# Taking one vector-matrix product off TensorE: ScalarE scales its rows, GpSimd adds them, and the weights are loaded later

## The chip, the cores and the metric

The kernel runs on one core of a Trainium2 chip. The metric is the device time of one execution, in microseconds; lower is better. All tensors are float32 in memory.

## The reference, cut to what matters

The program computes one layer of a hybrid attention block with a mixture of 32 experts, and behind it two layers of a second model, on 256 tokens of width 1024. The part that the change touches is the modulation:

```python
mod = (jax.nn.silu(c) @ w_ada + b_ada).reshape(b, 6, 1, 1024)
shift1, scale1, gate1, shift2, scale2, gate2 = (mod[:, i] for i in range(6))
h = rms_norm(x, norm1_g) * (1 + scale1) + shift1
x = x + gate1 * (y @ w_out)                       # y: the three mixers' output
h2 = rms_norm(x, norm2_g) * (1 + scale2) + shift2
```

`c` is one vector of 1024, `w_ada` is 1024 x 6144. The "second modulation" is columns 2048 to 4095 of the product: gate1 and shift2. gate1 is needed when the attention output has been projected, shift2 in the router and in the experts' inputs.

## The kernel before, in words

Every weight comes through a ring of 16 slots of 128x2048 floats (`ring`). `ring_order()` gives each load (a "unit") its slot; SyncE issues the loads in one fixed order (`fill`), each after waiting for what empties its slot (`emptied`). The slots 8 to 13 hold the split copies of the first stage and are not loaded into there; 14 and 15 are free until the experts.

The first stage ("front") computes `h @ w_in` in 32 pieces. A piece `n` is 256 rows of one block of columns: ScalarE makes its rounded high part (`hi`, in `his`), VectorE the rest (`lo`, in `los`, a subtraction of two SBUF inputs), and TensorE multiplies with both (`project(n)`, three products each, 12 to a half). `land(b)` copies a finished block out of PSUM. The attention mixers are woven between the pieces: `head_turn`, `cumulate` (the running sum of the forget gates `lf`), `sb_z`, `sb_r`, `sb_w` for the six stick-breaking heads, `fx_z`, `fx_t`, `fx_w` for the six forgetting heads. ScalarE and VectorE do their logarithms, exponentials and masks (`sb_beta`, `fx_mask`), GpSimd multiplies by the strict mask (`strict`) and by the convolution's taps (`tapped`). The order on each engine is written out by hand, an engine never goes on before its current wait is over, and counting semaphores (`done(name)`) join them.

The modulation is done in the same stage. `ada_unit(1, k, 7)` (TensorE) takes unit k: 128 rows of `w_ada`, 2048 columns. It multiplies four column quarters by one column of silu(c) (`cTp`, 32 wide, the rest zeros) into four partition groups of PSUM bank 7, summing over k. `mod_done(1, 7)` (VectorE) adds the bias, loaded by four small transfers of GpSimd's queue into `modr`. `mod_row` spreads gate1 over all partitions by a product with a selecting column, `strided` transposes turn shift2 into columns.

Behind the front come the output projection (`out_piece`), the router, and the experts, whose weights fill the rest of the ring. The four gate2 units sit in slots 8 to 11; they are loaded once piece 31 is used, and the loads `("w1", 1, 2)` and on, which take their slots, wait until TensorE has used them.

Of the kernel before, what the change touches and what calls it, by code (L numbers as in the profile page):

```python
# [118 lines left out]
STAGES = ["ada", "front", "oproj", "route", "moe", "moe2", "again", "mix", "ffn0", "pool", "ffn1", "last"]  # L119
LOADS = ["c", "const", "const2", "cumr", "x", "rows", "ab", "fb", "rb", "cw", "cwr", "vr", "gq", "rw", "ab2", "b1", "b2", "ps", "final", "out", "again", "w1_6", "w1_7"]  # L120

# [19 lines left out]
def front_order():  # L141

    order = [("modA", k) for k in range(4)] + [("in", 0, 0), ("in", 1, 0), ("modB", 0), ("modB", 1), ("in", 2, 0)]
    order += [("modB", 2), ("modB", 3), ("in", 0, 1), ("in", 1, 1)]
    units = [(2, 1)] + [(b, hf) for b in range(3, 8) for hf in range(2)]
    for n, mods in enumerate(((0,), (1,), (2, 3), (4, 5), (6, 7))):
        order += [("ada", 1, k) for k in mods] + [("in", *units[n])]
    return order + [("in", *u) for u in units[5:]]


def bank_before(b, t):

    users = [(c, s) for c in range(8) for s in range(2) if IN_BANKS[c][s] == IN_BANKS[b][t] and c < b]
    return users[-1] if users else None


def ring_order():
# [21 lines left out]
    for n, name in enumerate(order):  # L179
        if n == first:  # L180
            assert at % 2 == 0
            slots, at = [(at + i) % 8 for i in range(8)] + list(range(8, NRING)), 0
        if n == experts:
            slots, at = [14, 15, 12, 13, 0, 1, 2, 3, 4, 5, 6, 7, 8, 9, 10, 11], 0
        if n == post:
            slots, at = [14, 15, 0, 1, 2, 3, 4, 5, 6], 0
        s = slots[at % len(slots)]
        at += 1
        uses[s] += {"modA": 2, "modB": 2, "in": 3 if name[0] == "in" and name[1] >= 6 else 1}.get(name[0], 1)
        before = [prior[s]]  # L190
# [11 lines left out]
def build(nc, I, out, counts, counting):  # L202
    with ExitStack() as ctx:
# [32 lines left out]
        def held(name):  # L236

            c = name[2] % 2 if wide(name) else 0
            return (name[0], name[1], name[2] - c) if c else name, c

        def landed(name):
# [307 lines left out]
        def emptied(name):  # L549
# [17 lines left out]
            if kind == "w2":  # L567
                return [("w2", name[1], name[2] + wide(name)), ("w2b", name[1])]
            if kind == "dft":
                return [("width", 3)]  # L570
# [18 lines left out]
        def _(pe):  # L589
            P = sig["pe_ada"]  # L590

            def ada_unit(b, k, bank):
                u = rows_of(("ada", b, k), 1)
                pe.wait_ge(*landed(("ada", b, k)))
                for q in range(4):
                    i = pe.matmul(PS[32 * q:32 * q + 32, bank, :], cTp[:, k, :], u[:, 0, q * 512:(q + 1) * 512],
                                  start=k == 0, stop=k == 7)
                i.then_inc(*P.tick(("ada", b, k)))

# [111 lines left out]
            def sb_z(g):  # L711
                if g:
                    pe.wait_ge(*done("cumT"))
                    pe.wait_ge(*done("mod 1"))
                else:
                    pe.wait_ge(*done(("qk act", 0)))
                    pe.wait_ge(*done(("qk dve", 0)))
                nh = len(HEADS[g])
                for hh, h in enumerate(HEADS[g]):
                    for blk, (kb, qb) in enumerate(((0, 1), (0, 0), (1, 1))):  # L720
                        t = pe.matmul(Z[g][:, (blk * nh + hh) * 128:(blk * nh + hh + 1) * 128],
                                      KT[:, h // 2, kb * 128:(kb + 1) * 128], QZ[:, h, qb * 128:(qb + 1) * 128],
                                      start=True, stop=True)
                t.then_inc(*P.tick(("sz", g)))
# [83 lines left out]
            pe.wait_ge(*done("fB"))  # L808
            ada_unit(1, 0, 7)
            project(10, 11)  # L810
            ada_unit(1, 1, 7)
            project(12)
            ada_unit(1, 2, 7)
            ada_unit(1, 3, 7)
            head_turn(0, SQ)
            project(13)
            ada_unit(1, 4, 7)
            ada_unit(1, 5, 7)
            cumulate()
            project(14)  # L820
            sb_z(0)
            turn_cum()
            ada_unit(1, 6, 7)
            ada_unit(1, 7, 7)
            project(15)
# [21 lines left out]

            def mod_row(bank, v, half):
                f = v * 1024 + half * 512
                return pe.matmul(PS[:, bank, :], sel_w(f % 2048 // 512), modr[:, f // 2048, :], start=True, stop=True)  # L850

# [54 lines left out]
            for hf in range(2):  # L906
                for k in (2 + 2 * hf, 3 + 2 * hf):
                    pe.wait_ge(*done(("yL", k)))
                mod_row(6 + hf, 2, hf).then_inc(*P.tick(("gate1", hf)))
            out_piece(3)  # L910
# [33 lines left out]
            x_turn(1, 0)  # L944
            for cc in range(4):
                t = pe.transpose(PS[:, 0, cc * 128:(cc + 1) * 128], strided(modr[:, 1, :], cc), ident)
            t.then_inc(*P.tick("shift2 turned"))
# [684 lines left out]
        def _(dve):  # L1632
# [7 lines left out]
            def mod_done(b, bank):  # L1640
                last = {"A": ("modA", 3), "B": ("modB", 3), 1: ("ada", 1, 7), 2: ("scale2", 3), 3: ("gate2", 3)}
                at = {"A": 0, "B": 2, 1: 1, 2: 2, 3: 0}[b]
                dve.wait_ge(*done(last[b]))
                dve.tensor_tensor(modr[:, at, :], PS[:, bank, :], modr[:, at, :], ALU.add).then_inc(*V.tick(f"mod {b}"))
# [51 lines left out]
            for i in range(4):  # L1696
                dve.tensor_scalar(gq[i], PS[:, 0, 128 + i:129 + i], 1.0 if i % 2 else 0.125, None, ALU.mult).then_inc(
                    *V.tick("g8"))
            dve.wait_ge(s_load["ab"], 96)
            mod_done("A", 2)  # L1700
# [184 lines left out]
            h_low(6, 7)  # L1885
            los(8, 9)
            land(0)
            los(10, 11)
# [15 lines left out]
            cum_rows()  # L1904
            mod_done(1, 7)
            los(17)
# [80 lines left out]
            for n, (i, ns) in enumerate(((0, 0), (1, 0), (0, 1), (1, 1))):  # L1987
                xs = X[:, i, ns * 512:(ns + 1) * 512]
                if n == 3:
                    for h in range(2):  # L1990
# [15 lines left out]
            dve.wait_ge(*done("shift2 turned"))  # L2006
            dve.tensor_copy(sh2.rearrange("p (q c) -> p q c", q=2),
                            PS[:, 0, :].rearrange("p (c q z) -> p q c z", c=4, q=4)[:, 2:4, :, 0]).then_inc(*V.tick("s2"))
            dve.wait_ge(*done(("sd", "n2", 0)))
# [509 lines left out]
        def _(act):  # L2519
# [34 lines left out]
            def his(*pieces):  # L2554
                for n in pieces:
                    hi("in", n)

            def land(b):
                act.wait_ge(*done(("in", "first", b)))
# [97 lines left out]
            his(3, 4, 5, 6, 7)  # L2657
            h_high(4, 5, 6, 7)
            his(8, 9)
            land(0)  # L2660
            head_square(0, 0)
            his(10, 11)
# [3 lines left out]
            head_root(0)  # L2666
            his(13)
            forget_abs()
            land(2)
# [3 lines left out]
            forget_log()  # L2673
            his(15, 16, 17)
            sb_abs(0)
# [4 lines left out]
            sb_exp(1)  # L2680
            his(19, 20)
            sb_log(0)
            his(21)
# [4 lines left out]
            head_square(1, 1)  # L2688
            his(24)
            head_root(1)  # L2690
            land(5)
            his(25, 26, 27)
            sb_weight(0)
# [402 lines left out]
        def _(pool):  # L3096
# [17 lines left out]
            small("cw", cwr, I["conv_w"][0, :, :])  # L3114
            for q in range(4):
                small("ab", modr[32 * q:32 * q + 1, 1, :], I["b_ada"][:, 2048 + 512 * q:2560 + 512 * q])
            small("rb", rbrow, I["router_b"])
# [16 lines left out]
            pool.memset(KZ[64:66, 0:6:2, :], 1.0).then_inc(*G.tick())  # L3134
            pool.memset(KZ[0:2, 1:6:2, :], 1.0).then_inc(*G.tick("KZ zeroed"))
            pool.wait_ge(*done("KZ zeroed"))
            pool.wait_ge(*done("cumT"))
            for h in range(6):
# [26 lines left out]
            for g in range(2):  # L3165
                strict(g, ("sl", g), ("sa", g))
            pool.dma_start(rw.rearrange("p (m c) n -> p m (c n)", c=2),
                           I["router_w"][0].rearrange("(m p c) n -> p m (c n)", p=128, c=2)).then_inc(s_load["rw"], 16)
            for g in range(2):
                strict(g, ("se", g), ("sb", g))  # L3170
            for g in range(2):
                tapped(g)
# [68 lines left out]
        def _(sp):  # L3241
# [13 lines left out]

            def ada(b, k):
                fill_rows(("ada", b, k), I["w_ada"][0], k * 128, 1, b * 2048, 2048)

# [134 lines left out]
```

## Time and profile before

| | us |
|---|---|
| median of 3 runs | 1621.92 |
| lowest, highest | 1619.91, 1623.85 |
| the profiled execution, its own time | 1622.58 |
| its span in the profile | 1620.8 |
| TensorE busy | 1522.6 (94%) |
| VectorE, ScalarE, GpSimd busy | 669.7, 456.2, 113.7 |
| bytes moved by the transfers | 534.27 MB, mean 330 GB/s |

The profile's times start with the span. The front stage and the router take the first 190 us; the experts run to about 1120 us; the second model fills the rest. "Granted clock" is TensorE's clock as a share of its full speed.

### The profile page before, as it was taken

Reading aid. Unit: us, or ns where it says so; the run is one execution under the profiler, and the core shown is the slowest. Engines: PE = TensorE matmul, PEld = TensorE weight load, DVE = VectorE, ACT = ScalarE, POOL = GpSimd, SP = SyncE. Lnnn points to the kernel's source line nnn. Section 1 sums busy time; section 2 is a strip of 40 time slices with the busy share of each in tenths; the row PEclk is TensorE's granted clock in tenths of the full one; section 3 lists DMA queues with packets and bytes.
Section 4 is the critical chain, followed back from the end, with each engine's and each line's share of the span. In section 5 each row is a group of like instructions: output and inputs, shape, how many; then the busy total and the mean of one; then the engine's idle time right before and its main releaser. Section 6 shows DMA issues by size and latency. Waiting matters only on the chain.

```text
span 1620.8 us, 21577 instructions
## 1 busy us (share of the span) xinstructions
PE 1522.6 (94%) x8585; PEld 868.8 (54%) x8585; DVE 669.7 (41%) x969; ACT 456.2 (28%) x760; POOL 113.7 (7%) x125
## 2 busy tenths in 40 slices
PE   7999999999999998999998989887999999999998
PEld 4888533333333333333332323223858998899986
DVE  4676632323322232232222222224866665465654
ACT  3565311011101110111110110003765444454443
POOL 4132200000000000000000000000520002200000
PEclk9999999999999999999999999998999999999999
DMA  9977999999999999999999999999537555465520
GB/s 352 381 217 274 385 385 426 426 409 415 426 426 426 426 425 427 427 425 425 427 426 426 425 426 426 426 424 346 187 104 223 188 190 191 143 210 183 182 104 27
DMA packets 113394, 534.27 MB, mean 330 GB/s; under 512 B 7013, under 2 KB 70140, under 8 KB 87376
## 3 DMA queue, kind: packets, MB, share of 16 engines
q1 hardware_dynamic: 111232, 529.97, 82.6%
q8 instruction: 121, 1.98, 0.5%
q0 software_dynamic: 2000, 1.98, 0.4%
q14 instruction: 41, 0.34, 0.1%
HBM read 530.87 MB, written 1.05 MB: 328 GB/s over the span
## 4 chain that ended last, share of the span: by engine, by line
PE 43%; DMA 17%; DVE 4%; ACT 2%; issue 1%; DVEq 0%
DMA ring<-in_w_mlp 17%; PE ps L1021 8%; PE ps L576 8%; PE ps L578 8%; PE ps L577 8%; PE ps L1039 5%; PE ps L1046 1%; PE ps L1478 1%; PE ps L1469 1%; DVE ps L2364 1%; DVE wm L1638 1%; PE ps L992 1%; DVE arena L2139 0%; DVE arena L2132 0%; DVE arena L2135 0%
## 5 line engine op out<-in xcount | busy, mean ns | idle before, releaser
L1021 PE MATMUL ps<-ring,arena 128*64 128x512 f32 x2024 | 483.8, 603 | 20.2 <-DMA ring<-in_w_mlp 18.5
L1021 PEld LDWEIGHTS ps<-ring,arena 128*64 128x64 f32 x2024 | 129.1, 136 | 255.7 <-issue 210.4
L1039 PE MATMUL ps<-ring,arena 128*64 128x512 f32 x1024 | 231.0, 597 | 16.6 <-DMA ring<-in_w_mlp 10.3
L1638 DVE TENSOR_TENSOR wl<-ring,wh 128x1024 fp32r<-128x1024 f32 x132 | 161.9, 1232 | 136.1 <-ACT wh L2527 136.1
L576 PE MATMUL ps<-hth,wh 128*128 128x256 f32 x704 | 201.0, 285 | 0.9 <-DVE htl L2319 0.8
L577 PE MATMUL ps<-htl,wh 128*128 128x256 f32 x704 | 198.7, 282 | 0.0
L578 PE MATMUL ps<-hth,wl 128*128 128x256 f32 x704 | 198.1, 281 | 0.0
L2119 DVE TENSOR_TENSOR arena<-ps,arena 128x1024 f32<-128x1024 f32 x68 | 83.2, 1224 | 251.6 <-PE ps L1046 246.1
L2527 ACT ACTIVATE wh<-ring 128x1024 fp32r<-128x1024 f32 x132 | 139.3, 1060 | 148.9 <-PE ps L578 148.8
L1039 PEld LDWEIGHTS ps<-ring,arena 128*64 128x64 f32 x1024 | 75.2, 137 | 164.7 <-issue 140.4
L2144 DVE TENSOR_TENSOR arena<-ps,arena 128x512 f32<-128x512 f32 x34 | 23.5, 691 | 334.0 <-PE ps L1039 330.9
L577 PEld LDWEIGHTS ps<-htl,wh 128*128 128x128 f32 x704 | 135.7, 193 | 0.0
L578 PEld LDWEIGHTS ps<-hth,wl 128*128 128x128 f32 x704 | 134.7, 191 | 0.0
L576 PEld LDWEIGHTS ps<-hth,wh 128*128 128x128 f32 x704 | 133.7, 190 | 1.5 <-issue 1.0
L2795 ACT ACTIVATE arena<-arena 128x512 f32<-128x512 f32 (+1 forms) x33 | 20.4, 617 | 303.1 <-DVE arena L2132 303.1
L2816 ACT ACTIVATE obh<-arena 128x512 fp32r<-128x512 f32 x30 | 18.9, 630 | 288.9 <-DVE arena L2144 288.9
L577 PE MATMUL ps<-wl,fth 128*128 128x512 f32 x176 | 69.5, 395 | 0.0
L576 PE MATMUL ps<-wh,fth 128*128 128x512 f32 x176 | 69.5, 395 | 0.0
L578 PE MATMUL ps<-wh,ftl 128*128 128x512 f32 x176 | 69.4, 394 | 0.0
L3212 POOL TENSOR_TENSOR wm<-ring,wm 128x1024 fp32r<-128x1024 f32 x1 | 2.4, 2353 | 942.1 <-ACT wm L2527 942.1
L2776 ACT ACTIVATE arena<-ps,arena 128x256 f32<-128x256 f32 x60 | 30.6, 560 | 120.2 <-PE ps L992 115.2
L576 PE MATMUL ps<-wp,ht 128*128 128x384 f32 (+1 forms) x128 | 46.6, 364 | 2.9 <-DVE wp L1638 2.7
(457 smaller groups left out, 1851.4 us busy)
## 6 DMA issues: line engine op xcount, KB each, us to landing
ring<-in_w_mlp SPq DMA_DIRECT2D x187, 2048.0 KB, 27.5
ring<-in_ffn_w_gate SPq DMA_DIRECT2D x22, 1024.0 KB, 5.4
ring<-in_ffn_w_up SPq DMA_DIRECT2D x22, 1024.0 KB, 5.4
ring<-in_ffn_w_down SPq DMA_DIRECT2D x22, 1024.0 KB, 4.8
ring<-in_w_ada SPq DMA_DIRECT2D x16, 1024.0 KB, 9.5
ring<-in_w_ada SPq DMA_DIRECT2D x16, 512.0 KB, 11.2
ring<-in_w_mlp SPq DMA_DIRECT2D x8, 1024.0 KB, 33.1
ring<-in_w_in SPq DMA_DIRECT2D x10, 768.0 KB, 12.7
```

What stands on the lines that cost most here:

```text
L576: pe.matmul(o, lh, rh, start=first, stop=False)
L577: pe.matmul(o, lh, rl, start=False, stop=False)
L578: return pe.matmul(o, ll, rh, start=False, stop=last)
L1021: t = pe.matmul(PS[64 * g:64 * g + 64, HB[hb][ns], :], x[:, k8, :], u[:, f:f + 512], start=False, stop=k8 == 7)
L1039: t = pe.matmul(PS[64 * g:64 * g + 64, 3, :], a4[:, kc, 64 * kg:64 * kg + 64], u[:, c, g * 512:(g + 1) * 512], start=k8 == 0, stop=k8 == 7)
L1638: dve.tensor_tensor(l, src, h.bitcast(F32), ALU.subtract).then_inc(*V.tick((st, "lo", n)))
L2119: dve.tensor_tensor(x, PS[:, b:b + 2, :], x, ALU.add).then_inc(*tick(name))
L2144: dve.tensor_tensor(OBF, PS[:, bank, :], G2R, ALU.mult).then_inc(*tick(n_f))
L2527: act.activation(h, src, ACT.Copy).then_inc(*S.tick((st, "hi", n)))
L2776: act.activation(XGT[b % 2][:, k, :], PS[:, bank, (k % 2) * 256:(k % 2) * 256 + 256], ACT.Identity, scale=a2[:, k:k + 1], bias=sh2[:, k:k ...
L2795: act.activation(SIG[:, 0:n], GLU[:, 0:n], ACT.Sigmoid, scale=1.702).then_inc(*Q.tick(name))
L2816: act.activation(OBH[0], OBF, ACT.Copy).then_inc(*SM.same())
```

## The change

The eight units get the names `("ada", k)`. ScalarE multiplies unit k, 128x2048, by the k-th column of silu(c), one scalar for each partition: unit 0 into the ring's slot 15 (`row_sums`), the others in place. VectorE adds the bias, 1x2048, to partition 0 of the slot. GpSimd adds the units 1 to 7 to the slot, one after the other. The sum over the 128 partitions is left to TensorE: gate1 by a product with a matrix of ones, shift2 by eight products of a 128-column slice with a column of ones. The loads of the units move behind more of the `w_in` units. The bias comes in one transfer into slot 14. The experts' slots start with 12 and 13, and 14 and 15 come sixth and wait for shift2.

```diff
 def front_order():
-    for n, mods in enumerate(((0,), (1,), (2, 3), (4, 5), (6, 7))):
-        order += [("ada", 1, k) for k in mods] + [("in", *units[n])]
-    return order + [("in", *u) for u in units[5:]]
+    for n, k in enumerate((None, 0, 1, 2, 3, None, 4, 5, 6, 7, None)):
+        order += ([] if k is None else [("ada", k)]) + [("in", *units[n])]
+    return order
...
+GATE_SLOT = NRING - 1
 # ring_order, at the first expert
-            slots, at = [14, 15, 12, 13, 0, 1, 2, 3, 4, 5, 6, 7, 8, 9, 10, 11], 0
+            slots, at = [12, 13, 0, 1, 2, 3, 4, 5, 6, 7, 14, 15, 8, 9, 10, 11], 0
+            prior[GATE_SLOT] = ("row sums",)
 # emptied
+            if kind == "ada":
+                return [("summed", name[1])]
+            if kind == "row sums":
+                return ["shift2 turned"]
 # TensorE: ada_unit is gone, with its eight calls before and between
 # project(10) to project(15), and sb_z(1)'s wait for "mod 1"
-            def mod_row(bank, v, half):
-                f = v * 1024 + half * 512
-                return pe.matmul(PS[:, bank, :], sel_w(f % 2048 // 512), modr[:, f // 2048, :], start=True, stop=True)
+            def gate_row(half):
+                return pe.matmul(PS[:, 6 + half, :], ones, row_sums[:, half * 512:half * 512 + 512], start=True, stop=True)
-                mod_row(6 + hf, 2, hf).then_inc(*P.tick(("gate1", hf)))
+                pe.wait_ge(*done(("summed", 7)))
+                gate_row(hf).then_inc(*P.tick(("gate1", hf)))
-            for cc in range(4):
-                t = pe.transpose(PS[:, 0, cc * 128:(cc + 1) * 128], strided(modr[:, 1, :], cc), ident)
+            for k in range(8):
+                t = pe.matmul(PS[:, 0, k:k + 1], strided(row_sums[:, 1024:2048], k), ones[:, 0:1], start=True, stop=True)
 # VectorE, behind los(8, 9); mod_done(1, 7) is gone from behind cum_rows()
-            dve.wait_ge(s_load["ab"], 96)
+            dve.wait_ge(s_load["ab"], 32)
+            dve.wait_ge(*done(("ada scaled", 0)))
+            dve.wait_ge(s_load["ab1"], 16)
+            first = row_sums[0:1, :]
+            dve.tensor_tensor(first, first, ring[0:1, (GATE_SLOT - 1) * UNIT:GATE_SLOT * UNIT], ALU.add).then_inc(
+                *V.tick(("summed", 0)))
 # ScalarE: 0 before his(8, 9); 1 behind land(0); 2 behind his(13); 3 behind
 # his(15); 4 behind his(16); 5 behind his(19, 20); 6 behind his(24); 7 behind his(25)
+            def ada_scaled(*ks):
+                for k in ks:
+                    u = unit(("ada", k))
+                    act.wait_ge(*landed(("ada", k)))
+                    act.activation(u if k else row_sums, u, ACT.Copy, scale=cTp[:, k, 0:1]).then_inc(
+                        *S.tick(("ada scaled", k)))
 # GpSimd: 1 to 4 behind the memsets of KZ and before the wait for "cumT";
 # 5 behind the first strict products; 6 and 7 behind the second ones
-            for q in range(4):
-                small("ab", modr[32 * q:32 * q + 1, 1, :], I["b_ada"][:, 2048 + 512 * q:2560 + 512 * q])
+            small("ab1", ring[0:1, (GATE_SLOT - 1) * UNIT:GATE_SLOT * UNIT], I["b_ada"][:, 2048:4096])
+            def summed(k):
+                pool.wait_ge(*done(("ada scaled", k)))
+                pool.wait_ge(*done(("summed", k - 1)))
+                pool.wait_ge(*G.now())
+                pool.tensor_tensor(row_sums, row_sums, unit(("ada", k)), ALU.add).then_inc(*G.tick(("summed", k)))
```

## Rows read from the trace of the kernel before

**Rows 1.** Busy by stretches: from:to, us, busy (x instructions), clock, DMA share, GB/s.
```profile
60.00:70.00 10.00, 10.00 (x76) 6.21 (x68) 5.89 (x13) 7.05 (x13) 0.00 (x0) 1.00 1.02 404
...
200.00:400.00 200.00, 195.70 (x1009) 68.25 (x1007) 57.31 (x80) 23.41 (x44) 0.00 (x0) 1.00 0.98 412
...
800.00:1000.00 200.00, 178.88 (x865) 62.40 (x865) 48.68 (x64) 20.88 (x41) 0.00 (x0) 0.99 1.01 426
```

**Rows 2.** Timeline of SyncE's queue: start us, us, line, transfer.
```profile
33.13 1.73 SPq L3247 DMA_DIRECT2D ring<-in_w_in  x1
...
182.70 2.43 SPq L3247 DMA_DIRECT2D ring<-in_w_mlp  x2
```

**Rows 3.** Waits of SyncE's queue, 84 to 200 us: total, times, longest.
```profile
SPq L3246 <- PE ps L859: 25.8, 4, 16.0
```

**Rows 4.** Timeline of TensorE in the front.
```profile
55.24 0.45 PE L576 MATMUL ps<-wp,ht 128*128 128x390 f32 x1
...
70.31 0.39 PE L686 MATMUL ps<-arena 128*128 128x6 f32 x2
...
76.16 1.92 PE L596 MATMUL ps<-ring,arena 128*32 128x512 f32 x16
...
92.30 0.44 PE L576 MATMUL ps<-wp,ht 128*128 128x384 f32 x1
...
130.82 1.47 PE L776 MATMUL ps<-arena 128*128 128x128 f32 x12
```

**Rows 5.** Timeline of ScalarE: high parts of 768 and 1024 elements.
```profile
64.11 0.83 ACT L2527 ACTIVATE wp<-ring 128x768 fp32r<-128x768 f32 x1
...
137.74 1.04 ACT L2527 ACTIVATE wo<-ring 128x1024 fp32r<-128x1024 f32 x1
```

**Rows 6.** GpSimd's additions of line 3222: ns min/median/max, starts.
```profile
L3222 POOL TENSOR_TENSOR arena<-arena x24: 1263/1283/2101, 1149.1 to 1186.0; 128x512 f32<-128x512 f32 x24
```

**Rows 7.** Timeline of GpSimd: mask products.
```profile
91.53 2.98 POOL L3152 TENSOR_TENSOR arena<-arena 128x1024 f32<-128x1024 f32 x1 [5.03 <-DVE arena L1792]
...
107.64 2.36 POOL L3152 TENSOR_TENSOR arena<-arena 128x1024 f32<-128x1024 f32 x1 [9.31 <-ACT arena L2623]
```

**Rows 8.** Timeline of VectorE in the front.
```profile
47.90 1.81 DVE L1638 TENSOR_TENSOR wp<-ring,wp 128x768 fp32r<-128x768 f32 x2
...
69.27 0.17 DVE L1772 SCALAR_TENSOR_TENSOR arena<-arena 128x12 f32<-128x12 f32 x1 [0.85 <-ACT arena L2601]
...
87.83 1.76 DVE L1787 SCALAR_TENSOR_TENSOR arena<-ps,arena 128x1536 f32<-128x1536 f32 x1 [1.80 <-ACT arena L2619]
...
91.30 0.95 DVE L1638 TENSOR_TENSOR wp<-ring,wp 128x768 fp32r<-128x768 f32 x1
92.17 0.95 DVE L1787 SCALAR_TENSOR_TENSOR arena<-ps,arena 128x768 f32<-128x768 f32 x1
...
93.50 1.83 DVE L1638 TENSOR_TENSOR wp<-ring,wp 128x768 fp32r<-128x768 f32 x1
...
108.15 2.67 DVE L1638 TENSOR_TENSOR wp<-ring,wp 128x768 fp32r<-128x768 f32 x1
...
119.42 1.82 DVE L1809 TENSOR_TENSOR arena<-ps,arena 128x1024 f32<-128x1024 f32 x2 [1.17 <-PE ps L769]
```

**Rows 9.** Timeline of TensorE around shift2.
```profile
170.40 0.99 PE L928 MATMUL ps<-s,arena 128*128 128x2 f32 x8
...
174.21 0.64 PE L946 MATMUL ps<-arena 128*128 128x128 f32 x4
175.15 0.74 PE L939 MATMUL ps<-arena 128*128 128x128 f32 x4 [0.30 <-DVE arena L1995]
```

**Rows 10.** The load issued at 33.13 us: issue to landing, in us.
```profile
DMA to landing us min/median/max: 14.0/14.0/14.0
```

**Rows 11.** Busy by stretches at TensorE's two clocks.
```profile
26.00:28.00 2.00, 2.00 (x8) 2.00 (x8) 2.00 (x4) 2.00 (x5) 0.00 (x0) 0.50 1.06 385
...
34.00:36.00 2.00, 2.00 (x13) 2.00 (x12) 0.00 (x0) 0.00 (x0) 0.00 (x0) 1.00 1.06 383
```

More of the change, by code:

```diff
@@ L119 @@
 STAGES = ["ada", "front", "oproj", "route", "moe", "moe2", "again", "mix", "ffn0", "pool", "ffn1", "last"]
-LOADS = ["c", "const", "const2", "cumr", "x", "rows", "ab", "fb", "rb", "cw", "cwr", "vr", "gq", "rw", "ab2", "b1", "b2", "ps", "final", "out", "again", "w1_6", "w1_7"]
+LOADS = ["c", "const", "const2", "cumr", "x", "rows", "ab", "fb", "rb", "cw", "cwr", "vr", "gq", "rw", "ab1", "ab2", "b1", "b2", "ps", "final", "out", "again", "w1_6", "w1_7"]
 LAST_ALONE = tuple((NEXP - 1, k) for k in range(4, 8))
@@ L239, in held @@
             return (name[0], name[1], name[2] - c) if c else name, c
+        row_sums = ring[:, GATE_SLOT * UNIT:(GATE_SLOT + 1) * UNIT]
         def landed(name):
@@ L590, in _ @@
             P = sig["pe_ada"]
-            def ada_unit(b, k, bank):
-                u = rows_of(("ada", b, k), 1)
-                pe.wait_ge(*landed(("ada", b, k)))
-                for q in range(4):
-                    i = pe.matmul(PS[32 * q:32 * q + 32, bank, :], cTp[:, k, :], u[:, 0, q * 512:(q + 1) * 512],
-                                  start=k == 0, stop=k == 7)
-                i.then_inc(*P.tick(("ada", b, k)))
             def turn(src, m, bank, name):
@@ L713, in sb_z @@
                     pe.wait_ge(*done("cumT"))
-                    pe.wait_ge(*done("mod 1"))
                 else:
@@ L808, in _ @@
             pe.wait_ge(*done("fB"))
-            ada_unit(1, 0, 7)
             project(10, 11)
-            ada_unit(1, 1, 7)
             project(12)
-            ada_unit(1, 2, 7)
-            ada_unit(1, 3, 7)
             head_turn(0, SQ)
             project(13)
-            ada_unit(1, 4, 7)
-            ada_unit(1, 5, 7)
             cumulate()
@@ L822, in _ @@
             turn_cum()
-            ada_unit(1, 6, 7)
-            ada_unit(1, 7, 7)
             project(15)
@@ L1640, in mod_done @@
             def mod_done(b, bank):
-                last = {"A": ("modA", 3), "B": ("modB", 3), 1: ("ada", 1, 7), 2: ("scale2", 3), 3: ("gate2", 3)}
-                at = {"A": 0, "B": 2, 1: 1, 2: 2, 3: 0}[b]
+                last = {"A": ("modA", 3), "B": ("modB", 3), 2: ("scale2", 3), 3: ("gate2", 3)}
+                at = {"A": 0, "B": 2, 2: 2, 3: 0}[b]
                 dve.wait_ge(*done(last[b]))
@@ L1904, in _ @@
             cum_rows()
-            mod_done(1, 7)
             los(17)
@@ L2006, in _ @@
             dve.wait_ge(*done("shift2 turned"))
-            dve.tensor_copy(sh2.rearrange("p (q c) -> p q c", q=2),
-                            PS[:, 0, :].rearrange("p (c q z) -> p q c z", c=4, q=4)[:, 2:4, :, 0]).then_inc(*V.tick("s2"))
+            dve.tensor_copy(sh2, PS[:, 0, 0:8]).then_inc(*V.tick("s2"))
             dve.wait_ge(*done(("sd", "n2", 0)))
@@ L2658, in _ @@
             h_high(4, 5, 6, 7)
+            ada_scaled(0)
             his(8, 9)
             land(0)
+            ada_scaled(1)
             head_square(0, 0)
@@ L2667, in _ @@
             his(13)
+            ada_scaled(2)
             forget_abs()
@@ L2673, in _ @@
             forget_log()
-            his(15, 16, 17)
+            his(15)
+            ada_scaled(3)
+            his(16)
+            ada_scaled(4)
+            his(17)
             sb_abs(0)
@@ L2681, in _ @@
             his(19, 20)
+            ada_scaled(5)
             sb_log(0)
@@ L2689, in _ @@
             his(24)
+            ada_scaled(6)
             head_root(1)
             land(5)
-            his(25, 26, 27)
+            his(25)
+            ada_scaled(7)
+            his(26, 27)
             sb_weight(0)
@@ L3114, in _ @@
             small("cw", cwr, I["conv_w"][0, :, :])
-            for q in range(4):
-                small("ab", modr[32 * q:32 * q + 1, 1, :], I["b_ada"][:, 2048 + 512 * q:2560 + 512 * q])
+            small("ab1", ring[0:1, (GATE_SLOT - 1) * UNIT:GATE_SLOT * UNIT], I["b_ada"][:, 2048:4096])
             small("rb", rbrow, I["router_b"])
@@ L3135, in _ @@
             pool.memset(KZ[0:2, 1:6:2, :], 1.0).then_inc(*G.tick("KZ zeroed"))
+            def summed(k):
[3 more added lines that the diff above has]
+                pool.tensor_tensor(row_sums, row_sums, unit(("ada", k)), ALU.add).then_inc(*G.tick(("summed", k)))
             pool.wait_ge(*done("KZ zeroed"))
+            for k in range(1, 5):
+                summed(k)
+            pool.wait_ge(*G.now())
             pool.wait_ge(*done("cumT"))
@@ L3166, in _ @@
                 strict(g, ("sl", g), ("sa", g))
+            summed(5)
+            pool.wait_ge(*G.now())
             pool.dma_start(rw.rearrange("p (m c) n -> p m (c n)", c=2),
@@ L3170, in _ @@
                 strict(g, ("se", g), ("sb", g))
+            for k in (6, 7):
+                summed(k)
+            pool.wait_ge(*G.now())
             for g in range(2):
@@ L3254, in small, with ada @@
                 sp.dma_start(dst, src).then_inc(s_load[n], 16)
-            def ada(b, k):
-                fill_rows(("ada", b, k), I["w_ada"][0], k * 128, 1, b * 2048, 2048)
+            def ada(k):
+                fill_rows(("ada", k), I["w_ada"][0], k * 128, 1, 2048, 2048)
             def w_in(b, hf):
```

## The prediction

> **What bounds the kernel now.** I read the busy table by stretches first. TensorE fills every microsecond of 60 to 70 us, and from 200 us on the weights of the experts stream at 412 to 426 GB/s with a DMA share of 0.98 to 1.01 [rows 1]. So the span is a front stage set by TensorE's program order, and then a stream set by its start. Next I looked at where the stream starts: SyncE's queue issues the first load of expert 1 that needs a slot of gate2 at 182.70 us [rows 2], and it had waited up to 16.0 us for the products over gate2 [rows 3], which come last in the front. Everything issued before it has landed by then. A shift X of TensorE's front therefore shifts this issue, and the whole stream, by X: I take one for one. Last I read each engine's timeline from 30 to 140 us, because the edit lies there.
>
> **What is removed.** Eight units of the second modulation go. Two of them (16 records) take 1.92 us of TensorE ([rows 4], the row at 76.16), so eight take 7.7 us, all in a packed stretch. If nothing else moved, that would be the gain. VectorE also loses one addition of about 0.7 us (512 columns from PSUM).
>
> **What is added, each by its duration.**
> ScalarE: eight scalings of 128x2048. 768 elements take 0.83 us, 1024 take 1.04 [rows 5]; the slope of 0.21 per 256 gives 1.9 us each, 15 us in all.
> GpSimd: seven additions of 128x2048. 512 elements take 1.28 us [rows 6], 1024 take 2.36 [rows 7]; the slope gives 4.6, and I use 4.5 us each (ends: 4.3 by the slope of 2.1 ns alone, 5.1 by four times the small one), 32 us in all.
> VectorE: one addition of 1x2048. 768 columns take 0.95, 1536 take 1.76 [rows 8], so 2.3 us.
> The moved shift2: eight products with one column stand where four transposes stood (0.64 us [rows 9]). Four such products with two columns took 0.99 us [rows 9], so eight take 1.9. They end at 176.1 us where the next x transposes began at 175.15 after a wait of 0.30; the transposes after those waited for VectorE as well, so about +0.3 us of the delay is left. Ends: 0 and +1.3. The gate rows are the same two products of 512 columns as before: 0. Two bias loads fewer on GpSimd's queue at 11 us, the wait on 32 instead of 96, and the reordered slots of the experts: 0. Slots 14 and 15 now wait for shift2, which ends before the wait for gate2 that closes the stretch anyway; uncovered, such a wait would cost the 8 us between them.
>
> **The price that is not in these durations.** GpSimd's additions read SBUF, and so does VectorE's forming of the low parts (`lo`: two inputs in SBUF). Between 91.53 and 94.51 us GpSimd ran its mask product [rows 7]. VectorE's operations of that time show who is held [rows 8]: one with an input in PSUM took its usual 0.95; the low part that started at 93.50 ended at 95.33, 0.82 after GpSimd ended, where 0.95 from its start is usual. The low part at 108.15 took 2.67 and ended 0.8 after GpSimd's 107.64 + 2.36. The first GpSimd row waited in turn: 2.98 instead of 2.36, for the low part of 91.30. So whichever is second stands until the other is done. A low part that meets a 4.5 us addition is late by up to 4.5 us, and TensorE's next piece with it; where one is hidden depends on how early the low parts are.
> The Trainium skill, page "SBUF — State Buffer", section "Who interferes with whom", says that a VectorE instruction with two SBUF inputs contends with a GpSimd instruction that reads SBUF, and that the second fully blocks. By that rule, the trace agrees; without it the sum below would be +3, with it +8.5.
>
> **The replay, with pieces named as in the code.** Durations as above; unnamed operations keep theirs.
> (a) The first unit now goes behind ("in",2,1): it is the load issued at 33.13 us [rows 2], which landed 14.0 later [rows 10], at 47.1. ScalarE takes it before the high parts 8 and 9: 47.1 + 1.9 + 1.6 = 50.6. Low part 9 ends at 51.6, before at 49.7 [rows 8].
> (b) VectorE then adds the bias row: 53.9; landing of block 0, 54.4; ScalarE's square and high part 10, 56.0. GpSimd's addition 1 runs 53.9 to 58.4 and holds low part 10, which ends at 59.3. TensorE, done with piece 9 at 54.9, starts piece 10 at 59.3; before at 55.24 [rows 4]. The unit removed there (1 us) is already counted in this.
> (c) Low part 11, landing 1, square, low part 12, sum, root, norm and low part 13 follow by their durations: 67.4 (about 61.9 before). Scaling 2 ends at 67.2 on ScalarE, addition 2 runs 67.3 to 71.8 and holds low part 14 to 72.7. The head copies and the forget gate follow: `lf` at 75.2, before at 69.4 [rows 8]. TensorE's `cumulate` waits for it: 75.2 against 70.31 [rows 4], +4.9, with 5 us of idle before it.
> (d) TensorE now has 2 units fewer to do before piece 15, and regains 1.9: +3.0. Additions 3 and 4 hold low parts 16 and 17 to 81.9 and 87.3.
> (e) ScalarE has scalings 3, 4 and 5 (5.7 us) ahead of the logarithm that VectorE's `sb_beta(0)` needs: 94.2 against 87.83 [rows 8]. Low part 21 stands behind it on VectorE: 98.5 against 92.25. TensorE took piece 21 at 92.30, just as it came [rows 4]: there is no slack, so the shift is +6.2.
> (f) Addition 5 holds low part 24 to 110.1, just in time for TensorE's shifted 110. Scalings 6 and 7 lie partly in ScalarE's wait for head sums: +0.6.
> (g) Additions 6 and 7 hold low parts 28 and 29. The mask of the fox heads stands behind 29: in the old time's frame it moves from 119.42 [rows 8] to 124.8. Its exponentials are then done at 132.2 in that frame; TensorE asks for them at 130.82 [rows 4]: +1.4.
> Sum 6.2 + 0.6 + 1.4 + 0.3 = +8.5 us.
> (h) The idle stretches of (b) and (c) are 4 to 5 us. The granted clock of TensorE was 0.50 (1.2 GHz) at 26 to 28 us, where 8 products took 2 us, after a stretch in which the engine had little to do; at 34 to 36 us, at 1.00 (2.4 GHz), 13 did [rows 11]. A slow stretch of 6 us like the one from 24 us costs some 2.4 us. If it comes after `cumulate` it delays `sb_z(0)` and (e) with it; after (b) it is absorbed by the wait in (c). I take +1.5, ends 0 and +5.
> Together +10.0: the profiled execution's own 1622.58 becomes 1632.6. The median of the runs lies 0.66 below it, so 1632.
>
> **The rivals.**
> *GpSimd doesn't hold VectorE* (the two waits read above were something else, or the additions fall between the low parts). Then low part 10 ends at 56.9, `lf` comes at 71.7, and `sb_beta(0)` at 91.2 since ScalarE's scalings remain: +3.2, and +0.3 for shift2, less what is regained behind: +3, so 1625. Against it: three rows [rows 7, 8]. For it: small shifts of my replay move every meeting. Chance 0.16, most of it within 0.2%.
> *TensorE's time comes through.* The place is the stretch from 54 to 92 us. If ScalarE's scalings fall in its waits and the low parts stay ahead, the 7.7 us less appear at piece 21, less 1 us of (a) and the 0.3: 6.4, so 1615.5. It decides at `sb_beta(0)`: it would have to come at 81 to 82 us instead of 87.83, though ScalarE has 11 us more to do before it. For it: TensorE is the engine without gaps, ScalarE and VectorE are busy 7.05 and 5.89 of 10 us at 60 to 70 us [rows 1], so room exists on average. Against: they run in a fixed order, each waiting for the other. Chance 0.17.
> *The waits grow on each other.* Both slow stretches of (h), additions of 5.1 us, and a transfer of the out weights late because its slot waits for additions 6 and 7: +4 for the clock, +3 for the additions, +1: 1640. Chance 0.10.
> *Forecast:* 0.57.
>
> **How the numbers follow.** 0.2% (3.2 us, about what a measurement of this kernel can tell) is 1618.7 to 1625.2. Faster 0.18: the second rival and a sliver of the first. Same 0.12: most of the first. Slower 0.70: the forecast (its own range 1627 to 1638), the third, and the rest of the first. The range 1618 to 1641 leaves out the second rival and the far end of the third.
>
> **What would show it.** In the changed profile: GpSimd's additions at about 4.5 us, more where they wait; low parts on VectorE of 3 to 5 us, ending 0.8 after an addition; TensorE idle of several us before `cumulate`, released by VectorE; `sb_beta(0)` near 94 us; the gate2 loads and the first load behind them near 191 to 193 us instead of 182.70; the stream itself unchanged. I am wrong if `cumulate` comes before 70 us, or if low parts beside additions keep 0.95 us, or if the shift at piece 21 isn't found again at 182.70.

## The result, and the profile after

The change costs 21.5 us.

| | before | after |
|---|---|---|
| median of 4 runs, us | 1622.35 | 1643.86 |
| lowest, highest | 1619.91, 1623.85 | 1642.17, 1645.46 |
| ratio, with its 95% interval | | 1.0138 (1.0125 to 1.0151) |
| span of the profiled execution | 1620.8 | 1642.4 |
| TensorE, GpSimd busy | 1522.6, 113.7 | 1532.7, 145.9 |

The forecast was 1632 with a range to 1641: the right sign and, for the holds, the right mechanism, but half the size. TensorE is busy for 10 us more although it has 52 instructions fewer: its mean granted clock fell from 0.990 to 0.978. Between 50 and 180 us it was 1.00 throughout before; after the change it reads 0.50 (1.2 GHz) from 59 to 66, 76 to 84, 100 to 104 and 141 to 148 us.

Two points divide the time. The **front** ends where SyncE issues the four gate2 loads. The **router** ends where it issues the small load of line 3311 (3340 after), right behind the two loads of [rows 2] at 182.70 us. SyncE's queue before, then after:

```profile
134.43 2.23 SPq L3247 DMA_DIRECT2D ring<-in_w_ada  x4
...
185.19 0.94 SPq L3311 DMA_DIRECT2D arena<-in_w_mlp  x2
```

```profile
152.55 2.38 SPq L3276 DMA_DIRECT2D ring<-in_w_ada  x4
...
205.77 0.94 SPq L3340 DMA_DIRECT2D arena<-in_w_mlp  x2
```

Front +18.1, router 53.2 instead of 50.8 (+2.5), all behind it 1436.6 instead of 1435.6 (+1.0). The stream was only shifted, as forecast.

TensorE's waits after, from 0 to 230 us (total, times, longest), the waits for the first loads left out:

```profile
PE ps L586 <- DVE wp L1631: 7.0, 6, 4.3
...
PE ps L769 <- ACT arena L2635: 4.2, 1, 4.2
```

L586 is `project`, L769 `fx_z`. The first is the forecast hold of a low part. The label of the second misleads, as e11 shows. A third wait, 3.3 us, stands before `cumulate` (L688). The timelines of GpSimd, VectorE and TensorE after the change show the holds:

```profile
54.37 4.53 POOL L3155 TENSOR_TENSOR ring<-ring 128x2048 f32<-128x2048 f32 x1 [5.42 <-DVE ring L1883]
...
125.06 4.55 POOL L3155 TENSOR_TENSOR ring<-ring 128x2048 f32<-128x2048 f32 x1 [0.17 <-POOL arena L3176]
129.78 5.06 POOL L3155 TENSOR_TENSOR ring<-ring 128x2048 f32<-128x2048 f32 x1 [0.17 <-ACT wp L2523]
```

```profile
56.31 3.42 DVE L1631 TENSOR_TENSOR wp<-ring,wp 128x780 fp32r<-128x780 f32 x1 [1.71 <-ACT wp L2523]
...
98.16 1.76 DVE L1780 SCALAR_TENSOR_TENSOR arena<-ps,arena 128x1536 f32<-128x1536 f32 x1 [3.70 <-ACT arena L2623]
...
125.47 10.19 DVE L1631 TENSOR_TENSOR wp<-ring,wp 128x768 fp32r<-128x768 f32 x2
135.69 1.82 DVE L1802 TENSOR_TENSOR arena<-ps,arena 128x1024 f32<-128x1024 f32 x2
...
142.04 1.01 DVE L1794 COPY arena<-ps 128x512 f32<-128x512 f32 x2
```

```profile
59.88 0.66 PE L586 MATMUL ps<-wp,ht 128*128 128x390 f32 x1 [4.27 <-DVE wp L1631]
...
76.03 0.36 PE L688 MATMUL ps<-arena 128*128 128x6 f32 x2 [3.33 <-issue]
...
84.72 0.38 PE L695 MATMUL ps<-arena 128*6 128x128 f32 x2
...
143.20 1.19 PE L769 MATMUL ps<-arena 128*128 128x256 f32 x2 [4.22 <-ACT arena L2635]
...
148.94 1.47 PE L777 MATMUL ps<-arena 128*128 128x128 f32 x12
...
192.34 1.94 PE L939 MATMUL ps<-arena,ring 128*128 128x1 f32 x16
```

The low part that starts at 56.31 takes 3.42 us instead of the 0.95 or so of [rows 8] and ends at 59.73, 0.83 behind the addition. Two low parts stand 10.19 us behind the last two additions, and the fox mask (L1802) comes at 135.69 instead of 119.42 [rows 8]. Against [rows 4, 8]: piece 10 +4.6, `lf` +6.5, `cumulate` +5.7, `sb_beta(0)` +10.3, fox mask +16.3, `fx_t(0)` +18.1. Between `cumulate` and the transposes of its result (L695, L693 before) TensorE does the same products in both kernels, with no wait. They start 5.7 us later and end 8.9 us later:

```profile
75.85 0.38 PE L693 MATMUL ps<-arena 128*6 128x128 f32 x2
```

That row is the kernel before. The stretch took 5.54 us there (from 70.31) and takes 8.69 us now, at 0.50: the low clock costs 3.15 us here.

### The profile page after: what moved, and what is told of

Same layout as the page of the kernel before. It is cut to its first block, busy times and chain, and to the rows that moved or that the text cites. A ratio compares the mean times of both kernels' runs of the same rounds, so it can differ in the third digit from the quotient of the medians.

```text
span 1642.4 us, 21494 instructions
## 1 busy us (share of the span) xinstructions
PE 1532.7 (93%) x8533; PEld 881.7 (54%) x8533; DVE 691.6 (42%) x969; ACT 470.8 (29%) x768; POOL 145.9 (9%) x129
## 4 chain that ended last, share of the span: by engine, by line
PE 54%; DMA 13%; DVE 5%; ACT 2%; issue 1%; DVEq 0%
PE ps L1014 14%; DMA ring<-in_w_mlp 13%; PE ps L586 8%; PE ps L588 8%; PE ps L587 8%; PE ps L1032 8%; PE ps L1039 2%; PE ps L985 1%; DVE arena L2135 1%; DVE arena L2128 1%; DVE arena L2131 1%; PE ps L1471 1%; PE ps L1023 1%; DVE arena L2129 1%; PE ps L1462 1%
## 5 line engine op out<-in xcount | busy, mean ns | idle before, releaser
L586 PE MATMUL ps<-hth,wh 128*128 128x256 f32 x704 | 201.3, 286 | 0.9 <-DVE htl L2315 0.8
L1032 PEld LDWEIGHTS ps<-ring,arena 128*64 128x64 f32 x1024 | 75.8, 138 | 165.7 <-issue 140.8
L586 PEld LDWEIGHTS ps<-hth,wh 128*128 128x128 f32 x704 | 134.0, 190 | 1.5 <-issue 1.0
L586 PE MATMUL ps<-wh,fth 128*128 128x512 f32 x176 | 69.6, 396 | 0.0
L586 PE MATMUL ps<-wp,ht 128*128 128x384 f32 (+1 forms) x128 | 50.1, 392 | 9.1 <-DVE wp L1631 7.0
```

Source lines behind the costliest of these rows:

```text
L586: pe.matmul(o, lh, rh, start=first, stop=False)
L1032: t = pe.matmul(PS[64 * g:64 * g + 64, 3, :], a4[:, kc, 64 * kg:64 * kg + 64], u[:, c, g * 512:(g + 1) * 512], start=k8 == 0, stop=k8 == 7)
```

## The experiments

The ledger first (times in us; medians of before in the later groups of runs: 1622.58, 1622.0, 1622.24 and 1621.7). The columns front, router and behind are of the one profiled execution and add up to its span; the median is of all runs. The two differ most for e10 and e14: e10's profiled execution was the fastest of its ten (1623.51), e14's the slowest of its twelve (1624.82). A gate2 load is later or earlier by up to 2 us between kernels whose fronts do the same (after and e7: 152.55 and 150.69; e10 and e14: 135.32 and 137.07), so smaller steps of the front decide nothing alone. Most of this is the clock behind `cumulate`: the stretch that took 5.54 us before takes 8.69 after and 7.38 in e7, 7.07 in e10 and 8.69 in e14. Where sums are left incomplete, shift2 changes, and with it which expert a token takes; TensorE then has 8225 instructions (8379 in e5, 8687 in e2) instead of 8533, and in e8 8235 instead of the 8585 of before, of which only 42 are products that were cut. So for those the front and the router are read first, and the total second. In e3, e4 and e10 the part behind the router is also some 3.5 us shorter than in e1 and e14, which have as many instructions; why was not found.

| | gate2 loads at (front) | router | behind | median | ratio (interval) |
|---|---|---|---|---|---|
| before | 134.4 | 50.8 | 1435.6 | 1622.35 | |
| after | 152.6 | 53.2 | 1436.6 | 1643.86 | 1.0138 (1.0125, 1.0151) |
| e1 small additions | 140.8 | 50.8 | 1435.1 | 1628.89 | 1.0051 (1.0034, 1.0068) |
| e2 small scalings | 152.1 | 54.8 | 1454.8 | 1662.49 | 1.0252 (1.0235, 1.0269) |
| e3 both small | 140.0 | 54.7 | 1431.4 | 1627.88 | 1.0031 (1.0017, 1.0045) |
| e4 memsets | 140.4 | 53.3 | 1431.0 | 1628.32 | 1.0047 (1.0030, 1.0064) |
| e5 6 and 7 small | 145.1 | 54.9 | 1434.9 | 1637.48 | 1.0097 (1.0078, 1.0115) |
| e6 chunks | 143.0 | 53.4 | 1437.1 | 1634.96 | 1.0069 (1.0051, 1.0087) |
| e7 wide shift2 | 150.7 | 50.8 | 1434.9 | 1638.65 | 1.0101 (1.0084, 1.0118) |
| e8 before, few products | 135.1 | 50.8 | 1434.4 | 1620.84 | 0.9990 (0.9980, 0.9999) |
| e10 all small | 135.3 | 54.7 | 1431.7 | 1626.00 | 1.0026 (1.0015, 1.0036) |
| e11 so_kept first | 149.8 | 54.7 | 1435.0 | 1640.58 | 1.0111 (1.0093, 1.0128) |
| e12 chunks, wide, kept | 146.2 | 50.8 | 1437.0 | 1634.08 | 1.0069 (1.0054, 1.0083) |
| e13 the same, bias later | 147.9 | 50.8 | 1436.5 | 1635.08 | 1.0074 (1.0059, 1.0090) |
| e14 all small, wide | 137.1 | 50.7 | 1435.2 | 1622.35 | 0.9999 (0.9990, 1.0008) |
| e15 chunks, wide | 142.6 | 50.8 | 1436.4 | 1631.51 | 1.0058 (1.0041, 1.0074) |

**e1, e2, e3: which engine's added work costs.**

```diff
-pool.tensor_tensor(row_sums, row_sums, unit(("ada", k)), ALU.add)
+pool.tensor_tensor(row_sums[:, 0:32], row_sums[:, 0:32], unit(("ada", k))[:, 0:32], ALU.add)   # e1, e3
-act.activation(u if k else row_sums, u, ACT.Copy, scale=cTp[:, k, 0:1])
+act.activation(u[:, 0:32] if k else row_sums, u[:, 0:32] if k else u, ACT.Copy, scale=cTp[:, k, 0:1])   # e2, e3
```

> The changed kernel, but GpSimd's seven additions cover 32 of the 2048 columns (gate1 and shift2 are left mostly unsummed). Theory A (GpSimd's additions and VectorE's low parts exclude each other, and this is most of the loss): the low parts keep 0.95 us each, the fox mask is no longer late behind two of them, the clock drops less; what is left are ScalarE's scalings: 1627 (1622 to 1632). Theory B (ScalarE's 15 us of scalings set the loss): 1638 or more. Theory C (the new order of loads and the slots that wait for the sums set it): not told apart from A here, since the sums are also earlier.

> The changed kernel, but seven of ScalarE's eight scalings cover 32 of the 2048 columns (the first is whole; the units are summed mostly unscaled). The additions are whole. Theory A: the loss of the additions stays, about 4 us at the logarithm go: 1638 (1634 to 1642). Theory B: 1625 or less. Theory C: 1643.

> The changed kernel with both cuts: seven scalings and seven additions cover 32 columns. What is left is the missing work of TensorE, the new order of loads and slots, one whole scaling, the bias addition and the new shift2. Theories A and B: the 7.7 us of TensorE appear, less 2 for the first scaling and shift2: 1617 (1613 to 1621). Theory C: 1630 or more.

Additions of 32 columns take 11.7 us off the front; the low parts 10 and 11 (a pair like the one at 47.90 in [rows 8], 1.81 us) take 1.85 us together in e1, but 4.30 in e2. Small scalings take 0.5 to 0.8 us off it. e2's total isn't comparable: its experts do more work (behind the router 1454.8 us). e3 was expected at 1617 with the 7.7 us of TensorE coming through, and took 1627.88: a clear miss, which e8 and e10 take up.

**e4: is it GpSimd's time, or what it reads?** Each addition is replaced by three memsets of the unit (none reads SBUF), so its sums are left out.

> The changed kernel, but each of GpSimd's additions is replaced by three memsets of the same unit, 128x2048 (some 5.6 us, by 1.40 us for 1536 columns), which write SBUF and read nothing. GpSimd is as busy as with the additions and releases slots as late. Gate1 and shift2 are not summed. Theory A: the low parts on VectorE keep 0.95 us, so within 3 us of the run with small additions. Theory C, and any theory by which GpSimd's busy time delays its later work: 1643 or more.

GpSimd is as busy as after the change (152 us), yet the low parts run free. GpSimd and then VectorE in e4:

```profile
55.42 5.55 POOL L3156 MEMSET ring<- 128x2048 f32 x3 [7.00 <-DVE ring L1883]
```

```profile
57.40 1.85 DVE L1631 TENSOR_TENSOR wp<-ring,wp 128x780 fp32r<-128x780 f32 x2 [1.71 <-ACT wp L2523]
```

Two low parts stand wholly inside the memsets and take their usual 1.85 us. The front is that of e1 (140.4 and 140.8). So the order of instructions, the slots held longer and the loads behind them are not the cause of those 11.7 us: the additions' reading of SBUF is. By the rule of the Trainium skill, page "SBUF — State Buffer", section "Who interferes with whom", a GpSimd instruction that only writes does not contend with a VectorE instruction of two SBUF inputs; this trace agrees.

**e5: the last two additions.** Additions 6 and 7 have 32 columns.

> The changed kernel, but GpSimd's additions 6 and 7 cover 32 columns (units 6 and 7 are mostly left out of the sums); 1 to 5 are whole. Tests step (g) of the prediction. Theory A: low parts 28 and 29 are no longer held, the fox mask keeps its +11 us of before the step instead of +16.3, and the gate2 loads come at 152.55 - 6.5 = 146 us: 1637 (1635 to 1639). Rival (the five additions before set the whole shift, the last two fall into waits): 1643.

The front is 7.4 us shorter than after, of the 11.7 that all seven cost. Two of seven additions make most of the loss. TensorE's wait before `fx_z(1)` and the 0.50 from 141 to 148 us are gone with them; `fx_t(0)` starts at 141.51 instead of 148.94.

**e6: the same additions in pieces.** It computes the same.

```diff
+for n in range(8):
+    c = slice(256 * n, 256 * n + 256)
+    pool.tensor_tensor(row_sums[:, c], row_sums[:, c], unit(("ada", k))[:, c], ALU.add)
```

> The changed kernel with each addition of 2048 columns cut into eight of 256, all else equal. GpSimd's work grows from 4.5 to some 5.6 us an addition (0.7 each by the 0.75 of 128x256 in the profile before). Theory A, in the form that the hold lasts one instruction: a low part waits 0.7 us at most, so near the run with small additions: 1631 (1628 to 1636). Rival (a low part waits for the whole row of additions, or every piece is paid again by the next low part): 1642 or more.

VectorE gets in between two pieces: low part 29 takes 1.17 us where it stood behind a whole addition after the change. GpSimd pays with 6.4 to 7.5 us for an addition instead of 4.5 to 5.1. GpSimd, then VectorE, in e6:

```profile
121.80 7.01 POOL L3157 TENSOR_TENSOR ring<-ring 128x256 f32<-128x256 f32 x8 [0.17 <-POOL arena L3179]
```

```profile
124.98 1.17 DVE L1631 TENSOR_TENSOR wp<-ring,wp 128x768 fp32r<-128x768 f32 x1 [1.62 <-ACT wp L2523]
```

Most of the hold is gone (9.5 of 11.7 us of the front), 8.9 us of the total.

**e7: the products for shift2.** It computes the same.

```diff
-t = pe.matmul(PS[:, 0, k:k + 1], strided(row_sums[:, 1024:2048], k), ones[:, 0:1], start=True, stop=True)
+t = pe.matmul(PS[:, 0, 64 * k:64 * k + 64], strided(row_sums[:, 1024:2048], k), ones[:, 0:64], start=True, stop=True)
```

> The changed kernel, but shift2's eight products move 64 equal columns of ones each instead of one (same result, the first column is read). In the profile of the changed kernel the granted clock is 0.50 from 196 to 202 us, behind these products, and the router's part of the path grows from 48.3 to 50.7 us. If the few columns of these products bring the low clock, it is gone here and the time is 1.5 to 2 us lower: 1642. Rival (the low clock comes from elsewhere): clock again 0.50 there, 1644 to 1645.

The eight products take 1.99 us with 64 columns and 1.94 with one: narrowness saves nothing. But the clock behind them differs. The same stage by stretches (clock is the third number from the right), after the change and in e7:

```profile
194.00:196.00 2.00, 2.00 (x29) 1.86 (x28) 1.55 (x6) 2.00 (x7) 0.00 (x0) 0.94 0.94 262
196.00:198.00 2.00, 2.00 (x19) 0.82 (x19) 0.96 (x5) 1.97 (x6) 0.00 (x0) 0.50 0.71 279
```

```profile
196.00:198.00 2.00, 1.61 (x16) 0.94 (x20) 1.97 (x9) 1.98 (x3) 0.67 (x1) 1.00 0.94 393
```

With one column TensorE is at 1.2 GHz (0.50) from 196 us to past 202, though it was busy 4.00 of the 4 us up to 196, and the gate2 products there take 4.92 us instead of 3.64. In e7 it stays at 1.00. The ledger has it in every kernel: router 50.7 to 50.8 us in the five with wide products and in the two with the four transposes, 53.2 to 54.9 in eight of the nine with narrow ones; e1 kept the full clock and 50.8 all the same; why was not found. In e14, with wide products, the clock read 0.50 too, but only from 190 us on, behind the router, until about 193. The rest of e7's 5.2 us (front 1.9, behind 1.7) is within what repeats of one front and one stream differ by; 1.2 of the front's 1.9 were there at `sb_beta(0)` (96.99 instead of 98.16), behind the shorter slow stretch at `cumulate`.

**e8: what TensorE's 7.7 us were worth.** The kernel before, with the products of units 1 to 7 cut from four of 512 columns to one of 8: some 5.7 us of TensorE's time left out by its rows, with most of the sums (the expectation estimated 6.5).

> The kernel before, with the second modulation's products on TensorE cut: unit 0 whole, units 1 to 7 with one product of 8 columns each (the units are mostly left out of the sum). Some 6.5 us of TensorE's work are gone and nothing is added. Theory D (the front from 50 to 90 us is a chain through VectorE and ScalarE, and the products only filled TensorE's waits): 1622 (1620.5 to 1623), with idle on TensorE. Rival E (TensorE's work sets the front, as I took it): 1616 (1615 to 1618).

Front +0.7 us, total 0.1% less, at most 0.2% by its interval. Two things ate the time. TensorE in e8:

```profile
68.54 0.56 PE L687 MATMUL ps<-arena 128*128 128x6 f32 x2 [2.45 <-issue]
...
76.97 0.38 PE L694 MATMUL ps<-arena 128*6 128x128 f32 x2
```

First, the products filled waits. Five of the seven small units, 4.1 us less, stand before `cumulate`, but `lf`, which comes through ScalarE and VectorE, is only 1.0 us earlier (68.27 instead of 69.27), so TensorE stands 2.45 us and `cumulate` gains 1.8. Second, the granted clock is 0.50 from 68 to 75 us behind this idle time, where it was 1.00 before, and the same products take 8.43 us instead of 5.54: 2.9 us lost, more than was gained. `sb_beta(0)` comes at 88.51, 0.7 later than before. So e8 shows that the freed time was worth nothing here, not that the chain alone would have kept all of it. What it would be worth at a full clock no run shows.

**e10: all added work small.** Small additions, and also the first scaling and the bias addition; the last scaling stays wide. The sums are left incomplete.

```diff
+    c = slice(32, 2048) if k == 7 else slice(0, 32)
+    act.activation(row_sums[:, c] if k in (0, 7) else u[:, c], u[:, c], ACT.Copy, scale=cTp[:, k, 0:1])
+dve.tensor_tensor(first[:, 0:32], first[:, 0:32], ring[0:1, (GATE_SLOT - 1) * UNIT:(GATE_SLOT - 1) * UNIT + 32], ALU.add)
```

> The changed kernel with additions of 32 columns, as in the run with small additions, and now also the first scaling and the bias addition of 32 columns; only the last unit's scaling is wide (2016 columns, into the sums). So nearly all that the change adds on three engines is left out, and the sums are not the reference's; the order of the loads, the slots, the removed products and the narrow products for shift2 stay. It splits the +5.6 us of the front that were left with small additions and small scalings (140.0 against 134.4 us, at the first load of gate2). If they are the first scaling (2.0 us) and the bias addition (2.3 us) at the head of the chain through VectorE: that load at 134.4 to 135.5, total near 1623. If they are the order of the loads, the slots or the semaphores: at 139 to 140, total near 1628.

The front falls from 140.0 to 135.3, `sb_beta(0)` from 93.45 to 89.28 (87.83 before). The 4.2 us at `sb_beta(0)` are 3.0 at `lf` (73.22 to 70.19), which is the head of the chain, and 1.1 of the slow stretch behind `cumulate` (8.21 to 7.07 us). `lf` is 0.9 us later than before: so much is left at most for loads, slots and semaphores up to there. The median stays 3.8 us above before. The profile can't place these 3.8: the router has its 54.7 us, but this execution, the fastest of the ten, was only 0.9 us above the span of before. e14 tests the router.

**e11: what `fx_z(1)` waits for.** It computes the same.

```diff
 los(28, 29)
+so_kept(0)
+so_kept(1)
 ...
 los(31)
-so_kept(0)
-so_kept(1)
```

> The changed kernel with one thing moved on VectorE: the two copies of the strict heads' output out of PSUM (so_kept) stand ahead of the fox mask instead of behind it. It computes the same. If TensorE's 4.2 us of idle time before fx_z(1) at 143.2 us was a wait for these copies: fx_z(1) starts at about 139.5, the slow clock behind the idle time goes too, the first load of gate2 at 147 to 149 instead of 152.6 and the total 1637 to 1640 instead of 1643.9. If the idle time was a wait for ScalarE's exponentials, as the trace labels it, nothing moves: 1643 to 1645, as the mask then comes 1 us later.

`fx_z(1)` starts at 138.72 instead of 143.20, without a wait. The profile put the 4.2 us down to ScalarE's L2635 (an exponential); the code lets `fx_z(1)` wait for `so kept`, which VectorE did at 142.04 to 143.05, behind mask, maxima, a landing and two low parts. The gain reaches the front only as 2.7 us, since piece 30 then waits 2.19 us for its low part. The direction is as expected, the sizes fall short: load and total (149.81 and 1640.58) lie just outside the ranges given.

**e12 and e13: all remedies together.** Both compute the same.

> The changed kernel with additions in eight pieces of 256 columns, the products for shift2 moving 64 columns instead of one, and so_kept ahead of the fox mask. It computes the same. Chunks alone gave 1635.0, wide products alone 5.2 us less than the change. If the three add up: 1629 to 1631. If the wide products' gain was mostly noise of the front (their own part in the router was 2.4 us): 1632 to 1633.

> As the run before it, and the bias addition on VectorE (1x2048, 2.3 us) stands behind the copies of block 1 instead of before those of block 0. It computes the same. If the head chain is what is late: lf and cumulate 1.5 to 2.3 us earlier and the total 1 to 2 us below the run before it. If the unit's slot, which comes free some 6 us later, makes the next loads late: the pieces of blocks 5 and on come later, and the total is 1 to 4 us above it.

e12 missed. Where the low parts are on time, VectorE reaches `so_kept` early and stands 5.68 us for the products before it, with the fox mask behind: 133.52 instead of 127.11 in e6. One order is good only while VectorE is late. Moving the bias addition (e13) brought `lf` at 75.09 instead of 73.91, so not earlier, and gave 1635.08 against 1634.08, where the runs of the two overlap (1632.03 to 1636.91 and 1631.38 to 1635.64): no gain.

**e14 and e15: does the ledger close?** e14 is e10 with the wide products, e15 is e6 with them.

> As the run with all additions, the first seven scalings and the bias addition at 32 columns (the sums are not the reference's), and the products for shift2 moving 64 columns each instead of one. That run had the first load of gate2 0.9 us later than before, but 54.7 us from there to SyncE's first load behind gate2, against 50.8 before. If this is the narrow products and the 1.2 GHz behind them: 50.8 again, total 1622 to 1623, equal to the kernel before or 1 us above it although TensorE has 7.7 us less to do. If it is the changed slots or the order of loads: 53 to 55 again and total near 1626.

> The change with additions in eight pieces of 256 columns and products for shift2 of 64 columns, so_kept where the change has it. It computes the same. If the costs add up: 1635.0 (chunks alone) less 2.5 (the narrow products' share in the router): 1631.5 to 1633.5, still 10 us above the kernel before. If the moved so_kept was not what cost 3 us in the run that had all three: 1634 as there.

e14's median equals the kernel before, with 3.65 us less than e10: the wide products are worth that in the total. No gain is there for the 7.7 us that TensorE lost, as in e8: TensorE stands 3.97 us before `cumulate`, and the stretch behind it takes 8.69 us instead of 5.54. Its instructions behind the router are also fewer, so a cost of a microsecond or two could hide in this equality; its front was 2.7 us later. e15 computes the same as the change at 12.3 us less; it is the fastest complete form tried, and still 9.8 us above before.

## Why the prediction was wrong

Confirmed: the shift of SyncE's queue one for one; scalings (2.0 against 1.9), additions (4.53 to 5.08 against 4.5), the bias addition (2.27 against 2.3); and the hold itself (e1, e4), with its 0.8 us tail. (a), (b) and (c) hold: piece 10 at 59.88 against 59.3, `cumulate` at 76.03 against 75.2.

**Step (d) to (e), too small.** `sb_beta(0)` came at 98.16, not 94.2, though `lf` was only 0.7 later than forecast. The rest lies behind the wait at `cumulate`. From there to ScalarE's first step on the product of `sb_z(0)`, TensorE stood nowhere, and the low clock from 76 to 84 us added 3.15: (h) named the place and priced it at 1.5. From that step to `sb_beta(0)` it took 1.5 us longer, about one of ScalarE's scalings (the fifth, 1.99 us at 93.23); the third and fourth fell into its wait for TensorE, so the 5.7 us of step (e) were too much. The 1.9 us that (d) regains lie behind the product of `sb_z(0)` and don't help this path. In e10, with a like idle time (3.97 us) but with free low parts and small scalings, the slow stretch cost 1.5 and the shift grew by only 0.5 us from `lf` to `sb_beta(0)`.

**Step (g), the failing one.** It let the fox mask slip by 5.4 us and followed only one consumer, the exponentials, to reach +1.4. In the measured frame the mask slipped 16.3, of which 11.0 were there at the strict mask's product (118.60 against 107.64 [rows 7]): so the slip itself was forecast (5.3). But VectorE's copies `so_kept` stand behind the mask, and TensorE's `fx_z(1)` waits for them with less slack: before, the copies ended at 126.8 us and `fx_z(1)` began at 127.4. The step charged the hold to the instruction that was looked at, not to all that is queued behind it. From `sb_beta(0)` on, (f) and (g) were +2.0; measured was 18.1 - 10.3 = +7.8: 0.6 up to `fx_z(0)`, 4.9 at `fx_z(1)`, behind its wait of 4.2, and 2.3 from there to `fx_t(0)`, the same products without idle time, at 0.50 until 147.5. e5 confirms the additions, e11 the wait.

**The moved shift2, mis-sized.** Its longer duration cost nothing, as said (+18.1 us both at `fx_t(0)` and at the norm products behind shift2). What follows them did: +2.5 us of the router at 1.2 GHz, of which the text had nothing, as it looked at idle stretches only (e7, e14).

**The sum.** (a) to (c) +0.7, (d), (e) and (h) together +1.9, (f) and (g) +5.8, router +2.1, the stream +1.0 beyond the forecast: 11.5 of the 11.6 us between +10.0 and +21.6. Counted across the steps, stretches at 1.2 GHz make some 8 of the 21.6: 3.15 behind `cumulate`, 2.3 behind `fx_z(1)`, 2.5 in the router; (h) had 1.5.

A slip without effect: three bias loads fewer are on GpSimd's queue, not two (four became one).

**The rivals.** "TensorE's time comes through" is refuted by e8 and e14; it wanted `sb_beta(0)` at 81 to 82, and e8 has 88.51. "GpSimd doesn't hold VectorE" is refuted by e4 beside e1; its number, 1625, was too low even for free holds (1628 in e1 and e4), because `sb_beta(0)` came at 94.79 in e1 instead of that rival's 91.2: `lf` 1.0 later than it said, and 2.8 us of low clock behind `cumulate`. "The waits grow on each other" was nearest: its clock, 1.5 + 4, is the 5.5 us of the two slow stretches in the front, though the second of them came at `fx_z(1)` and not behind (b), and its transfers played no part.

## What to carry to other kernels

Time of the busiest engine is worth something only where that engine is the one that comes last; shrink its work in the kernel as it is (e8) before building the replacement. Idle time made on that engine can cost more than itself: here each variant had 2.5 to 4.7 us of it before `cumulate`, and 1.5 to 3.2 us of low clock behind. When an instruction is delayed on an in-order engine, list everything queued behind it and find the consumer with the least slack among all of those. Where GpSimd reads SBUF while VectorE has two-input work on the critical chain, try it in pieces of about a low part's length, which gave back 9.5 of 11.7 us here (e6).

## What the runs showed that was not expected

- TensorE's granted clock was 0.50 behind its idle time at `cumulate` in the changed kernel and in every variant, e8 too; in the kernel before, without that idle time, it stayed at 1.00. The same products took 7.07 to 8.69 us instead of 5.54.
- Eight float32 products (16 records) took 1.94 us with 1 moving column and 1.99 with 64, and behind the narrow ones the granted clock fell to 0.50 for 7 to 10 us in eight kernels of nine, with TensorE busy all the while ahead of the fall (4.00 of 4 us after the change).
- Cutting a 4.5 us addition of GpSimd into eight of 256 columns made it 6.4 to 7.5 us long, but took 9.5 us off the front.
- A memset of 128x2048 by GpSimd took 1.85 us and held no low part; an addition of that size took 4.53 to 5.08 us and held the low parts that met it.
